# Sixteen conditioning slabs moved beside the latent attention, and the whole first feed-forward in seven products

## The chip, the cores and the metric

One core of one Trainium2 chip runs the kernel as a single program. The metric is the device time of one execution in microseconds (us); lower is better. Nothing is shared with other cores: all inputs come from HBM and the output goes back there.

## The reference, cut to what matters

The reference is two transformer-like blocks on one sequence of T = 512 tokens of width 1024, all in float32. What this change touches is the first block:

```
mod = silu(c) @ ada_w[layer] + ada_b[layer]          # per layer: 1024 -> 6 * 1024, "conditioning"
shift_m, scale_m, gate_m, shift_f, scale_f, gate_f = split(mod, 6)
h = rmsnorm(x, g) * (1 + scale_m) + shift_m
y = gated_delta_mixer(h) if layer == 0 else latent_attention(h)      # GDN / MLA
x = x + gate_m * y
h = rmsnorm(x, g2) * (1 + scale_f) + shift_f
x = x + gate_f * (silu(h @ w_gate) * (h @ w_up)) @ w_down            # D_FF = 2816
```

The second block (retention, sliding-window attention, a third feed-forward) follows and is not changed. The conditioning is a product of one row vector with a 1024 x 6144 matrix per layer: 24 slabs of 256 columns per layer, 48 in all, 1 MB each.

## The kernel before, in words

Everything is kept with channels on the 128 partitions and the 512 tokens along the free dimension. Weights come as slabs of 128 x 2048 float32 (1 MB), two in flight: `raw[0]`, `raw[1]`. Each slab is split into a rounded high half (`hi`, on ScalarE, `split_hi` L358) and the rest (`lo`, on VectorE, `split_lo` L364: raw minus hi, both in SBUF), and a product is three matmul passes, lo*H, hi*L, hi*H (`product`, L301 to L303). Semaphores order the engines: `lo_ready` counts split slabs, `slab_done` finished products, `bank_free` emptied accumulators. SyncE issues all DMAs in one written order: `load_slab` (L533) waits until the slab two before has been split, `load_ada` (L539) until PE has summed the conditioning slab two before it. A wait in that list holds back everything behind it.

A conditioning slab goes this way (`ada_chunks`, L369): DMA into `adar[0]` or `adar[1]`; GpSimd multiplies the 128 x 2048 tile by silu(c) (L373), then adds it up in three halvings, 1024, 512 and 256 wide (L375); PE sums the 128 partitions with two products against a column of ones (`ada_pe`, L523 to L531), each two passes, into columns of accumulator `D[3]`; VectorE adds the bias later (`mod_dve`) and makes the gains (`gain_cols`). Eight slabs of 48 are done at the start by another way, 40 by this one, numbered 2 to 41. Twenty run in the delta mixer, 2 to 21 (`ada_pool`, five per pair of heads, each pair's gated by VectorE), two are multiplied during its output product, and twenty, those two among them, are summed by PE one behind each of the first twenty slabs of the first feed-forward (numbers 22 to 41).

Each feed-forward has 34 slabs: 14 gate/up slabs, 8 down slabs, 8 gate/up slabs, 4 down slabs. The second and the third do the first two gate/up slabs as plain products and the other 12 and 8 by a Strassen-like scheme (`seven_pe`, L1709): seven quarter products of the slab halves and sums of halves, each 4 x 3 matmuls of 256 columns, plus extra splits, copies and sums on ScalarE and VectorE (`quick_pe`, `quick_act`, `quick_dve`). It needs the sums of the activations in `tH` and `tL`. In the first feed-forward (`ffn_pe` L2052, `ffn_act`, `ffn_dve`) only the last 8 gate/up slabs go that way; its first 14 are plain products, because `tH` lies in the same memory as `adar`, which is still in use by the conditioning.

Around it: `final_pe` (L594) is the output product of a mixer or the last down slabs of a feed-forward, with the squares of x for the next norm beside it. `close_act` and `close_dve` (L779) make the normed activation chunk by chunk and half by half: `nq` = x * gain * rstd (L789), `hH` on ScalarE, `hL` = `nq` + shift - `hH` (L796); PE's first product of the next stage (`product_halves`, L333 to L335) takes the chunks as they come. Before the attention, `mla_in_dve` computes the rope angles (L2136 to L2147), splits a slab, normalizes the latent (`craw`, `cL`, L2217, L2221) and turns the keys and queries (L2495 to L2497, L2531 to L2533).

The latent attention (`mla_pe` L2244) has 4 pairs of heads with 8 units each (2 heads x 4 blocks of queries). PE runs for each unit scores, then fills of the next pair's projections (`fill`), then the transpose of the probabilities of two units before (`turn`), then the values of three before. VectorE makes the maxima (from PSUM) and scales the probabilities (`pr` L2526); ScalarE makes the exponentials. Its last units alternate `turn`, `fill(1)` and `values`, where the fills are pieces of the output product's first slab.

## Time and profile before

| what | us |
| --- | --- |
| median of 3 runs (lowest, highest) | 2343.72 (2341.77, 2344.22) |
| the profiled execution, its own time | 2343.12 |
| its span, first to last instruction | 2341.3 |
| PE busy in the span | 2261.8 (97%) |
| DVE, ACT, POOL busy | 1397.7, 1034.7, 366.9 |

PE is TensorE's matmuls, PEld its weight loads, DVE VectorE, ACT ScalarE, POOL GpSimd and SP SyncE. POOL works in the first third of the span only. Stages, in us from the span's start: delta mixer to 425, its output product to 473, first feed-forward 473 to 850 (its plain gate/up slabs to 642, down to 723, sevens to 805, last down slabs behind), closing norm and latent input to 912, attention to 1046, its output product to 1081, second feed-forward 1081 to 1442. The mean granted clock of the core is 0.993.

### The profile page before, as it was taken

The numbers are of one execution on the slowest core, as the hardware profiler recorded it, in microseconds if no ns is written. First come the engines' busy times: TensorE is split into PE (matmuls) and PEld (weight loads), VectorE is DVE, ScalarE is ACT, GpSimd is POOL, SyncE is SP. The second block draws the span as 40 slices with busy tenths as digits, with TensorE's granted clock in tenths as the row PEclk, the third lists the DMA queues.
The fourth block names the chain that finished last, engine by engine and source line by source line (L and its number), as shares of the span: only waits on it lengthen the run. The fifth ranks groups of instructions, "written<-read, shape, count | busy, mean of one in ns | idle before, by whom it ended". The sixth has DMA issues, their size and how long they took to land.

```text
span 2341.3 us, 34757 instructions
## 1 busy us (share of the span) xinstructions
PE 2261.8 (97%) x14301; PEld 1916.9 (82%) x14301; DVE 1397.7 (60%) x1792; ACT 1034.7 (44%) x1545; POOL 366.9 (16%) x164
## 2 busy tenths in 40 slices
PE   6999999999999999999999999999999999999998
PEld 4777888888889986668998998888777788998897
DVE  4856755543347764546883676645467435984484
ACT  4546553443214544435552445334355324553352
POOL 0346447347790000000000000000000000000000
PEclk9999999999999999999999999999999999999999
DMA  7433232324452324311323232222211222233232
GB/s 293 149 113 136 100 135 91 118 117 180 180 210 90 114 73 162 126 64 63 104 105 116 90 127 97 90 72 72 90 55 55 85 96 73 91 109 126 90 109 90
DMA packets 40762, 260.56 MB, mean 111 GB/s; under 512 B 4432, under 2 KB 6832, under 8 KB 10416
## 3 DMA queue, kind: packets, MB, share of 16 engines
q1 hardware_dynamic: 40624, 258.59, 30.4%
q8 instruction: 103, 1.69, 0.3%
q14 instruction: 35, 0.29, 0.0%
HBM read 256.42 MB, written 2.15 MB: 110 GB/s over the span
## 4 chain that ended last, share of the span: by engine, by line
PE 79%; DVE 8%; ACT 5%; issue 2%; POOL 2%; DMA 0%; DVEq 0%; ACTq 0%
PE D L301 10%; PE D L302 10%; PE D L303 10%; PE D L1692 7%; PE D L1694 7%; PE D L1693 7%; PE D L1457 2%; PE D L2941 2%; PE D L1459 2%; PE D L1458 2%; DVE lo L366 1%; PE D L2943 1%; PE D L2942 1%; PE D L1476 1%; ACT hi L362 1%
## 5 line engine op out<-in xcount | busy, mean ns | idle before, releaser
L366 DVE TENSOR_TENSOR lo<-raw,hi 128x2048 fp32r<-128x2048 f32 (+3 forms) x131 | 290.0, 2214 | 198.8 <-ACT hi L362 198.6
L362 ACT ACTIVATE hi<-raw 128x2048 fp32r<-128x2048 f32 (+3 forms) x131 | 230.1, 1757 | 327.7 <-PE D L303 239.7
L301 PE MATMUL D<-hH,lo 128*128 128x512 f32 x560 | 227.9, 407 | 6.1 <-DVE lo L366 6.1
L303 PE MATMUL D<-hH,hi 128*128 128x512 f32 x560 | 221.3, 395 | 0.0
L302 PE MATMUL D<-hL,hi 128*128 128x512 f32 x560 | 221.3, 395 | 0.0
L1692 PE MATMUL D<-tH,lo 128*128 128x256 f32 x768 | 217.0, 283 | 0.5 <-issue 0.5
L1694 PE MATMUL D<-tH,hi 128*128 128x256 f32 x768 | 216.8, 282 | 0.0
L1693 PE MATMUL D<-tL,hi 128*128 128x256 f32 x768 | 216.5, 282 | 0.0
L375 POOL TENSOR_TENSOR adar<-adar 128x1024 f32<-128x1024 f32 (+2 forms) x120 | 212.4, 1770 | 9.4
L373 POOL TENSOR_TENSOR adar<-adar,small 128x2048 f32<-128x2048 f32 x40 | 154.9, 3874 | 324.9 <-DVE zi L1343 186.7
L1692 PE MATMUL D<-hH,lo 128*128 128x256 f32 x576 | 163.1, 283 | 2.3 <-ACT D L1775 2.3
L1694 PE MATMUL D<-hH,hi 128*128 128x256 f32 x576 | 162.6, 282 | 0.0
L1693 PE MATMUL D<-hL,hi 128*128 128x256 f32 x576 | 162.3, 282 | 0.0
L301 PE MATMUL D<-aH,lo 128*128 128x512 f32 x390 | 154.6, 396 | 0.0
L302 PE MATMUL D<-aL,hi 128*128 128x512 f32 x390 | 154.1, 395 | 0.0
L303 PE MATMUL D<-aH,hi 128*128 128x512 f32 x390 | 154.0, 395 | 0.0
L1692 PEld LDWEIGHTS D<-tH,lo 128*128 128x128 f32 x768 | 144.9, 189 | 1.1 <-issue 0.8
L1693 PEld LDWEIGHTS D<-tL,hi 128*128 128x128 f32 x768 | 145.0, 189 | 0.2
L1694 PEld LDWEIGHTS D<-tH,hi 128*128 128x128 f32 x768 | 144.8, 189 | 0.0
L301 PEld LDWEIGHTS D<-hH,lo 128*128 128x128 f32 x560 | 105.9, 189 | 33.5 <-DVE lo L366 7.9
L302 PEld LDWEIGHTS D<-hL,hi 128*128 128x128 f32 x560 | 105.8, 189 | 25.5 <-issue 2.4
L303 PEld LDWEIGHTS D<-hH,hi 128*128 128x128 f32 x560 | 105.6, 189 | 24.6
(547 smaller groups left out, 5438.8 us busy)
## 6 DMA issues: line engine op xcount, KB each, us to landing
raw<-in_slabs SPq DMA_DIRECT2D x185, 1024.0 KB, 4.8
adar<-in_ada SPq DMA_DIRECT2D x42, 1024.0 KB, 4.8
fw<-in_ada SPq DMA_DIRECT2D x6, 1024.0 KB, 23.3
x<-in_xin SPq DMA_DIRECT2D x2, 1024.0 KB, 8.9
dt<-bcast SPq DMA_DIRECT2D x8, 256.0 KB, 3.2
dtb<-bcast SPq DMA_DIRECT2D x8, 256.0 KB, 3.4
qd<-bcast SPq DMA_DIRECT2D x8, 256.0 KB, 3.6
out<-x SPq DMA_DIRECT2D x8, 256.0 KB, 2.2
```

What stands on the lines that cost most here:

```text
L301: T_.matmul(o, lo[s.slot][:, w], H[:, k, :], start=(k == 0), stop=False)
L302: T_.matmul(o, hi[s.slot][:, w], L[:, k, :], start=False, stop=False)
L303: last = T_.matmul(o, hi[s.slot][:, w], H[:, k, :], start=False, stop=(k == kc - 1))
L362: S_.activation(hi[s.slot][:, 0:n], raw[s.slot][:, 0:n], ACT.Copy).then_inc(hi_ready, 1)
L366: V_.tensor_tensor(lo[s.slot][:, 0:n], raw[s.slot][:, 0:n], hi[s.slot][:, 0:n], ALU.subtract).then_inc(lo_ready, 1)
L373: chain.link(nc.gpsimd.tensor_tensor(r3, r3, cact.unsqueeze(2).to_broadcast([P, KC, 2 * P]), ALU.mult))
L375: last = nc.gpsimd.tensor_tensor(r3[:, 0:n], r3[:, 0:n], r3[:, n:2 * n], ALU.add)
L1457: T_.matmul(o, lo[s % 2][:, c], hH[:, k, :], start=(k == 0), stop=False)
L1458: T_.matmul(o, hi[s % 2][:, c], hL[:, k, :], start=False, stop=False)
L1692: T_.matmul(to, w(lo, k), H(k), start=(fresh and k == 0), stop=False, skip_group_check=True)
L1693: T_.matmul(to, w(hi, k), L(k), start=False, stop=False, skip_group_check=True)
L1694: last = T_.matmul(to, w(hi, k), H(k), start=False, stop=(k == 3), skip_group_check=True)
```

## The change

Only slabs 22 to 25 of the conditioning are now summed by PE in the output product of the delta mixer. All that is left, 26 to 41 (parts of the second layer that its attention output and its feed-forward need), is loaded, multiplied and added up from the last down slabs of the first feed-forward on, through the closing norm, the latent input and the attention. The halvings end in a tile of their own, `adas`, which moves the attention's tiles up by 16 KB per partition, so that a load waits for GpSimd (`ada_sum`) and no more for PE. PE sums the sixteen in two groups of eight between the last units of the attention, and the four fill pieces move behind. The first feed-forward becomes `quick_*` with f = 0: 12 more slabs by seven products. The bias and the gains of the late parts are made behind the attention.

```diff
+ADA_MLA = 8 + 4 * ADA_P + 4 - ADA_SKEW
...
         mla = ExitStack()
+        adas = sb("adas", [P, 16, 2 * P], scope=mla)
...
-        def ada_chunks(pool, chain, a):
+        def ada_chunks(pool, chain, a, to=None):
...
+            for n in (4, 2):
+                chain.link(nc.gpsimd.tensor_tensor(r3[:, 0:n], r3[:, 0:n], r3[:, n:2 * n], ALU.add))
+            nc.gpsimd.tensor_tensor(r3[:, 0:1] if to is None else to, r3[:, 0:1], r3[:, 1:2],
+                                    ALU.add).then_inc(ada_sum, 1)
...
-            def body(i):
-                for j in range(2):
-                    ada_chunks(pool, chain, Slab(ADA0 + n + j, i, 2))
-            loop(pool, (2 * ADA_L - 8 - n) // 2, body, chain, 6)
+            for a in range(ADA0 + GH // 2 * ADA_P, ADA_MLA):
+                ada_chunks(pool, chain, Slab(a))
+            for k in range(16):
+                ada_chunks(pool, chain, Slab(ADA_MLA + k), adas[:, k:k + 1])
...
+        def ada_late_pe(pe, k):
+
+            pe.wait_ge(ada_sum, ADA_MLA + k + 1 - ADA0)
+            for m in range(2):
+                c = 3 * P + 2 * k + m
+                last = T_.matmul(D[3][:, 0, c:c + 1], adas[:, k, m * P:(m + 1) * P], ones[:, 0:1], start=True, stop=True)
+            last.then_inc(ada_done, 1)
...
         def load_ada(sp, a):
-            if a.b >= 2:
+            if a.b >= ADA_MLA + 2:
+                sp.wait_ge(ada_sum, a.plus(-1 - ADA0))
+            elif a.b >= ADA_MLA:
+                sp.wait_ge(slab_done, Slab(G_MIN - N_OUT - 1).plus(1))
+            elif a.b >= 2:
                 sp.wait_ge(ada_done, a.plus(-1))
...
-        def final_pe(pe, base, kc, H, L, ready, f, begun=False):
+        def final_pe(pe, base, kc, H, L, ready, f, begun=False, also=lambda j: None):
             for j in range(N_OUT - 1):
                 s = Slab(base + j)
+                also(j)
...
             for h in range(2):
+                also(N_OUT - 1 + h)
...
-        Q7 = lambda f, part: 2 * (N7[1] + (f - 1) * sum(N7) + part * N7[0])
-        RUN = lambda f, part: 2 * f + part - 1 if f else 0
+        Q7 = lambda f, part: 2 * (f * sum(N7) + part * N7[0])
+        RUN = lambda f, part: 2 * f + part
...
             g = base + NORD
+            if f == 0:
+                act.wait_ge(ada_done, ADA_MLA)
             diff_hi(act, f, 0)
...
-        def ffn_pe(pe, base, f, hb, n, ada_base=None):
...
             def turn(g):
-                w("pn", g + 1)
                 if g >= 2:
                     w("pt", g - 1)
+                w("pn", g + 1)
...
             turn(UALL - 1)
-            fill(1)
+            w("pt", UALL - 1)
+            for k in range(8):
+                ada_late_pe(pe, k)
             values(UALL - 2)
-            fill(1)
+            for k in range(8, 16):
+                ada_late_pe(pe, k)
             values(UALL - 1)
+            fill(2)
             fill(2)
...
-            ada1 = ADA0 + GH // 2 * ADA_P
+            load_ada(sp, Slab(ADA_MLA - 4))
+            load_ada(sp, Slab(ADA_MLA - 3))
             load_slab(sp, Slab(G_GOUT + 2))
+            load_ada(sp, Slab(ADA_MLA - 2))
             load_slab(sp, Slab(G_GOUT + 3))
-            load_ada(sp, Slab(ada1))
-            load_ada(sp, Slab(ada1 + 1))
-            load_slab(sp, Slab(G_FFN0))
-            load_slab(sp, Slab(G_FFN0 + 1))
-            left = 2 * ADA_L - ADA_SKEW - ada1 - 2
-            both(G_FFN0 + 2, ada1 + 2, left // 2, 2, (1, 1))
-            g = G_FFN0 + 2 + left
-            alone(g, G_MLA - g)
+            load_ada(sp, Slab(ADA_MLA - 1))
+            alone(G_FFN0, N_FFN)
+            late = iter(range(ADA_MLA, ADA_MLA + 16))
+            load_ada(sp, Slab(next(late)))
+            load_ada(sp, Slab(next(late)))
+            for j in range(N_MIN):
+                load_slab(sp, Slab(G_MIN + j))
+            load_ada(sp, Slab(next(late)))
+            load_ada(sp, Slab(next(late)))
             for p in range(GH // 2):
                 for k, src in enumerate((1, 0, 2, 3)):
                     load_slab(sp, mla_slab(p, k), G_MLA + PAIR * p + src)
+                    if (p, k) not in ((0, 0), (0, 2), (1, 0), (1, 1)):
+                        load_ada(sp, Slab(next(late)))
...
-            final_pe(pe, G_GOUT, KC, hH, hL, h_batch(pe, 1), 0)
-            ffn_pe(pe, G_FFN0, 0, 2, 1, ADA0 + GH // 2 * ADA_P)
+            final_pe(pe, G_GOUT, KC, hH, hL, h_batch(pe, 1), 0,
+                     also=lambda j: ada_pe(pe, Slab(ADA_MLA - 4 + j - j // 2 + j // 4), 1) if j != 2 else None)
+            quick_pe(pe, G_FFN0, 0, 1)
...
             def second_layer():
-                mod_dve(dve, chain, 6 * KC, 12 * KC, 2 * ADA_L - ADA_SKEW)
+                mod_dve(dve, chain, 6 * KC, 8 * KC, ADA_MLA, D[3][:, 1, 6 * KC:8 * KC])
                 dve.wait_ge(mod_ready, 2)
                 gain_cols(chain, 2, "mix_g", 1, 1)
-                gain_cols(chain, 3, "ffn_g", 1, 4)
-            ffn_dve(dve, chain, G_FFN0, 0, gate_col(0, 5), second_layer)
+            quick_dve(dve, chain, G_FFN0, 0, gate_col(0, 5), second_layer)
...
             mla_dve(dve, chain, 4)
+            mod_dve(dve, chain, 8 * KC, 12 * KC, ADA_MLA + 16, D[3][:, 0, 3 * P:3 * P + 4 * KC])
+            dve.wait_ge(mod_ready, 3)
+            gain_cols(chain, 3, "ffn_g", 1, 4)
             final_dve(dve, G_MOUT, gate_col(1, 2), 2)
```

## Rows read from the trace of the kernel before

**Rows 1.** The page, busy time, share and instructions of each engine.
```profile
PE 2261.8 (97%) x14301; PEld 1916.9 (82%) x14301; DVE 1397.7 (60%) x1792; ACT 1034.7 (44%) x1545; POOL 366.9 (16%) x164
```

**Rows 2.** Windows: stretch, length, busy PE, PEld, DVE, ACT, POOL, clock, DMA, GB/s.
```profile
491.05:837.03 345.98, 345.52 (x1855) 296.96 (x1855) 169.10 (x155) 118.04 (x128) 164.69 (x72) 1.00 0.41 155
1099.41:1426.18 326.77, 324.84 (x2212) 300.00 (x2213) 224.37 (x270) 148.38 (x217) 0.00 (x0) 1.00 0.30 107
```

**Rows 3.** Timeline of PE: start, duration, line, tiles, [idle before <- releaser].
```profile
437.27 0.50 PE L301 MATMUL D<-hH,lo 128*128 128x512 f32 x1 [0.60 <-DVE lo L366]
459.69 0.28 PE L611 MATMUL D<-hH,lo 128*128 128x256 f32 x1
502.34 0.50 PE L529 MATMUL D<-cst,adar 128*128 128x1 f32 x4
513.93 0.50 PE L529 MATMUL D<-cst,adar 128*128 128x1 f32 x4
```

**Rows 4.** Timeline of PE, end of the attention.
```profile
1044.53 0.50 PE L2248 MATMUL D<-hH,lo 128*128 128x512 f32 x1 [1.41 <-DVE hL L2509]
```

**Rows 5.** Timeline of POOL, one conditioning slab beside the first feed-forward.
```profile
519.39 3.60 POOL L373 TENSOR_TENSOR adar<-adar,small 128x2048 f32<-128x2048 f32 x1 [2.08 <-DMA adar<-in_ada]
523.07 4.57 POOL L375 TENSOR_TENSOR adar<-adar 128x1024 f32<-128x1024 f32 x3
```

**Rows 6.** Timelines of POOL and DVE where both work, delta mixer.
```profile
110.09 0.69 DVE L1360 COPY egl<-qd 128x8 f32<-128x8 f32 x1
314.87 3.61 POOL L373 TENSOR_TENSOR adar<-adar,small 128x2048 f32<-128x2048 f32 x1
315.37 4.18 DVE L1261 SCALAR_TENSOR_TENSOR qs<-qs,fs 128x1024 f32<-128x1024 f32 x1
359.11 3.60 POOL L373 TENSOR_TENSOR adar<-adar,small 128x2048 f32<-128x2048 f32 x1
361.43 4.63 DVE L1315 TENSOR_TENSOR go<-go,qs 128x512 f32<-128x512 f32 x2
365.99 3.35 DVE L366 TENSOR_TENSOR lo<-raw,hi 128x2048 fp32r<-128x2048 f32 x1
```

**Rows 7.** Windows over the delta mixer's output, the close, one attention pair.
```profile
425.10:437.20 12.10, 11.57 (x49) 8.83 (x47) 8.83 (x14) 8.59 (x12) 0.00 (x0) 1.00 0.07 31
848.95:877.85 28.90, 26.14 (x159) 22.73 (x157) 26.56 (x52) 17.63 (x28) 0.00 (x0) 1.00 0.10 37
952.00:984.40 32.40, 31.27 (x158) 21.68 (x158) 18.22 (x51) 13.15 (x35) 0.00 (x0) 1.00 0.38 130
```

**Rows 8.** Timelines of PE, SP and POOL: what sets when a slab arrives.
```profile
419.67 0.50 PE L529 MATMUL D<-cst,adar 128*128 128x1 f32 x4
437.62 0.91 SPq L542 DMA_DIRECT2D adar<-in_ada  x2
444.36 3.60 POOL L373 TENSOR_TENSOR adar<-adar,small 128x2048 f32<-128x2048 f32 x1 [35.15 <-DMA adar<-in_ada]
841.84 0.34 SPq L536 DMA_DIRECT2D raw<-in_slabs  x1
877.88 0.33 SPq L536 DMA_DIRECT2D raw<-in_slabs  x1
895.32 0.33 SPq L536 DMA_DIRECT2D raw<-in_slabs  x1
```

**Rows 9.** Timeline of DVE with POOL idle.
```profile
425.11 1.29 DVE L1315 TENSOR_TENSOR go<-go,qs 128x512 f32<-128x512 f32 x2 [1.93 <-ACT go L1093]
863.65 2.28 DVE L366 TENSOR_TENSOR lo<-raw,hi 128x2048 fp32r<-128x2048 f32 x1
885.66 2.08 DVE L2217 SCALAR_TENSOR_TENSOR craw<-craw,vec,pr 128x512 f32<-128x512 f32 x3 [4.20 <-ACT pr L2180]
904.27 0.69 DVE L2497 TENSOR_TENSOR qr<-qr,craw 128x512 f32<-128x512 f32 x1
942.71 0.49 DVE L2526 TENSOR_SCALAR pr<-pr,small 128x512 f32<-128x512 f32 x1
```

More of the change, by code:

```diff
@@ L373, in ada_chunks @@
             chain.link(nc.gpsimd.tensor_tensor(r3, r3, cact.unsqueeze(2).to_broadcast([P, KC, 2 * P]), ALU.mult))
-            for n in (4, 2, 1):
-                last = nc.gpsimd.tensor_tensor(r3[:, 0:n], r3[:, 0:n], r3[:, n:2 * n], ALU.add)
-                if n > 1:
-                    chain.link(last)
-            last.then_inc(ada_sum, 1)
+            for n in (4, 2):
+                chain.link(nc.gpsimd.tensor_tensor(r3[:, 0:n], r3[:, 0:n], r3[:, n:2 * n], ALU.add))
+            nc.gpsimd.tensor_tensor(r3[:, 0:1] if to is None else to, r3[:, 0:1], r3[:, 1:2],
+                                    ALU.add).then_inc(ada_sum, 1)
         def ada_pool(pool, chain):
-            n = GH // 2 * ADA_P
-            for k in range(n):
+            for k in range(GH // 2 * ADA_P):
                 if k % ADA_P == 0:
@@ L840, in gain_cols, with mod_dve @@
                 in1=vec[:, V[src] + KC * layer:V[src] + KC * layer + KC], op0=ALU.add, op1=ALU.mult))
-        def mod_dve(dve, chain, lo_, hi_, ada_n):
+        def mod_dve(dve, chain, lo_, hi_, ada_n, cols):
             dve.wait_ge(ada_done, ada_n)
-            V_.tensor_tensor(mod[:, lo_:hi_], D[3][:, 1, lo_:hi_], vec[:, V["ada_b"] + lo_:V["ada_b"] + hi_],
+            V_.tensor_tensor(mod[:, lo_:hi_], cols, vec[:, V["ada_b"] + lo_:V["ada_b"] + hi_],
                              ALU.add).then_inc(mod_ready, 1)
@@ L2049, in quick_dve @@
             final_dve(dve, g + 2 * N7[1], gate, 2 * f + 1)
-        def ffn_pe(pe, base, f, hb, n, ada_base=None):
-            hidden = lambda off, also: lambda k: hidden_pe(pe, 11 * f + off, k, also)
-            linear_pe(pe, base, N_GUA, KC, 2, hH, hL,
-                      lambda s: product_halves(pe, s, hb, {3: lambda: ones_half(pe, n - 1, 1)}), ada_base)
-            for j in range(N_DNA):
-                s = Slab(base + N_GUA + j)
-                if j == 0:
-                    product_first(pe, s, FA, 1, aH, aL, hidden(0, {}))
-                else:
-                    product(pe, s, FA, 1, aH, aL)
-                if ada_base + N_GUA + j < 2 * ADA_L - ADA_SKEW:
-                    ada_pe(pe, Slab(ada_base + N_GUA + j), 1)
-            base += N_GUA + N_DNA
-            close = sevens_pe(pe, base, Q7(f, 1), N7[1], lambda k: pe.wait_ge(h_ready, h_base(hb) + 2 * KC + k))
-            final_pe(pe, base + N_GUB, FB, aH, aL, hidden(FA // 2, {1: close}), n)
@@ L2068, in ffn_act @@
-        def ffn_act(act, base, f, nf):
-            def body(i):
-                s = Slab(base, i, 2)
-                act.wait_ge(slab_done, s.plus(1))
-                S_.activation(sg[:], D[s.slot][:], ACT.Silu).then_inc(bank_free[s.slot], 1)
-                split_hi(act, s.next(2))
-                u = s.next()
-                act.wait_ge(bank_free[u.slot], u.prior(1))
-                S_.activation(aH[:, bass.ds(at(0, i, 2), 2), :], af[:], ACT.Copy).then_inc(aH_ready, 1)
-                split_hi(act, u.next(2))
-            loop(act, N_GUA // 2, body)
-            g = base + N_GUA
-            for j in range(N_DNA - 2):
-                split_hi(act, Slab(g + j + 2))
-            act.wait_ge(ada_done, 2 * ADA_L - ADA_SKEW)
-            for k in range(4):
-                diff_hi(act, f, k)
-            g += N_DNA
-            before_act(act, g, Q7(f, 1))
-            sevens_act(act, g, Q7(f, 1), N7[1], 0)
-            final_act(act, g + N_GUB, nf)
@@ L3229, in _ @@
                     row_in(sp, qd, 2, p + 1, "eg_in")
-            def both(g, a, n, per, ada_per):
-                def body(i):
-                    k = 0
-                    for j in range(per):
-                        load_slab(sp, Slab(g + j, i, per))
-                        for _ in range(ada_per[j]):
-                            load_ada(sp, Slab(a + k, i, sum(ada_per)))
-                            k += 1
-                loop(sp, n, body)
             def alone(g, n):
@@ L3340, in _ @@
             close_act(act, G_GOUT, 0, 1, col(mod, MD(0, 3)))
-            ffn_act(act, G_FFN0, 0, 1)
+            quick_act(act, G_FFN0, 0, 1)
             close_act(act, G_MIN - N_OUT, 1, 2, col(mod, MD(1, 0)))
@@ L3369, in _ @@
             gdn_dve(dve, chain)
-            mod_dve(dve, chain, 2 * KC, 6 * KC, ADA0 + 2 * KC)
+            mod_dve(dve, chain, 2 * KC, 6 * KC, ADA0 + 2 * KC, D[3][:, 1, 2 * KC:6 * KC])
             dve.wait_ge(mod_ready, 1)
```

32 lines of the change are left out of this document (removed).

## The prediction

> **What bounds the kernel now.** First the page's busy shares: PE is busy for 97% of the span [rows 1], so a change gains what it takes from PE's stream and loses what it makes PE wait. Then I lay windows over stages, to compare the first feed-forward with the second, which already has the form that the first is to get [rows 2]. Then PE's own timeline, for the price of one product slab and of one column sum [rows 3]. Last POOL and DVE side by side, because the change moves POOL's work from a place where DVE is half idle to places where it isn't: the reader should see that two engines that never wait on each other by a semaphore still lengthen each other's instructions [rows 6].
>
> **The first feed-forward.** From the start of its second slab to its last down slabs it takes 345.98 us; the same stretch of the second takes 326.77 [rows 2]. The difference, 19.2, is the gain. It can be split. A plain product takes (459.69 - 437.27)/2 = 11.21 us; with a column sum behind it the pitch is 513.93 - 502.34 = 11.59, so a sum costs 0.38 [rows 3]. Twenty sums leave this stage, nineteen in the stretch: 7.2. The remaining 12.0 is 12 slabs by seven products, 1.0 each. DVE and ACT get more work there (224 and 148 us of 327 in the second), which leaves both below PE [rows 2], and SP's loads become those of the second.
>
> **Column sums that come back.** Four sums go into the delta mixer's output product. One falls into the wait before its second slab (0.60, for `lo`) [rows 3]; three are paid: 1.1. Sixteen stand at the end of the attention, 6.1, in place of the fill pieces, which now stand behind the last values and cover the wait of 1.41 for `hL` that is there now [rows 4]; I count 1.3 of it and take 4.8. The two tiny DVE operations of `mod_dve` and `gain_cols` go with this: they lie beside the fills. The exchange of the two waits in `turn` changes no order of work. So far -19.2 + 1.1 + 4.8 = -13.3.
>
> **What a conditioning slab does to DVE.** One slab is four POOL instructions, 3.60 for the product and 4.57 for the three halvings, 8.1 us in all when nothing disturbs it [rows 5]. The halvings take 2.4, 1.3 and 0.8 of it. Where DVE wants to read two tiles from SBUF meanwhile, it stands still until POOL's instruction is over: `qs<-qs,fs` started at 315.37, half a microsecond into a POOL product of 3.61, and took 4.18. Two products `go<-go,qs` took 4.63 at 361.43, against 1.29 for the pair with POOL idle, and the split behind them 3.35 against 2.28 [rows 6, 9]. Three DVE instructions in a row were each held up by a different POOL instruction. They take turns, one instruction each. So in a gapless run of such DVE operations, POOL's whole 8.1 us per slab is added to DVE's chain, less only DVE's idle time. A copy of 8 columns with a single SBUF input took 0.69, as long as a full 512 columns elsewhere [rows 6, 9], so it was held too; operations with an input in PSUM are the ones that I take as free. The nearest other reading is that the delay falls on POOL; that bounds the cost at zero. I take DVE, by these rows.
>
> By the Trainium skill ("SBUF — State Buffer", section "Who interferes with whom") a VectorE instruction with two SBUF inputs and a GpSimd instruction that reads SBUF exclude each other for the whole instruction, whichever came first. By that rule the turns would be the same; the trace agrees, with the 4.18 at 315.37.
>
> **Where the moved slabs fall.** (a) Delta mixer's output. The load of slab 23 waits for PE's sum of slab 21 at 419.67; a transfer takes some 5 us, so POOL starts near 425. Slab 24 may load as soon as PE has summed 22, at 425, and follows at once. Before, POOL was idle until 444.36 [rows 8]. DVE from 425.10 until PE gets its split at 437.2 is busy for 8.83 of 12.10 with `go`, `hL` and the split, nearly all of two SBUF inputs, and PE has no gap to give [rows 7, 3]. Two slabs hold 16.2, DVE's idle time takes 3.3: +12.9. Bounds 0 and 16.2.
>
> (b) Close and latent input. The loads of 28 and 29 stand right behind the raw load at 841.84. In the same constellation (issued at 437.62 behind a raw load) POOL began at 444.36, 6.7 us later [rows 8]; here that is 848.95. From there to 877.85 DVE is busy for 26.56 of 28.90 with `nq`, `hL`, a split, the rope angles and the split that PE's third slab needs [rows 7]. 16.2 - 2.3 = +13.9. PE has 2.8 of idle time in the same stretch, which is DVE's waiting already. Bounds 0 and 16.2. Slabs 26 and 27 come before it, beside the last down slabs, where a product lasts 11.2 us [rows 3] and a split of 2.3 [rows 9] has room: nothing, at most the 16.2 of the others.
>
> (c) Latent norm. The load of 30 follows the raw load at 877.88, and POOL starts near 885, just as DVE makes `craw` (three operations at 885.66) and then `cL` [rows 8, 9]. 8.1 less some 2.6 of slack before PE wants `cL`: +5.5. The load of 31 follows that at 895.32 and reaches POOL near 902.5, into the turning of keys and queries (0.69 each), where PE waits for DVE anyway; three of the four POOL instructions catch an operation: +5.0 [rows 8, 9]. Bounds 0 and 16.2 together.
>
> (d) Attention, ten slabs. In a pair DVE is busy for 18.22 of 32.40 [rows 7]: 14.2 idle. Fourteen operations per pair read SBUF only: four splits, two of the query turning, eight of `pr` (at most 0.49) [rows 9]. For the `pr` scalings no row shows a collision; the one-input copy is the nearest [rows 6], and I count them in. A random arrival while POOL runs finds, over pieces of 3.6, 2.4, 1.3 and 0.8, a mean rest of 1.3, so 14 x 1.3 = 18.2 per pair, 4.0 more than DVE has. Three pairs: +12. Bounds: 0, where all of it fits into the idle time, and 80.5 - 3 x 14.2 = 38, where every turn is lost.
>
> The skill's same section says that `copy`, `cast` and `tensor_scalar` can enter a two-port mode that excludes GpSimd too. By it the count of 14 would stand; were it not so, six operations would remain, 7.8 per pair, less than DVE's idle time, and (d) would be near nothing, 2367 in all. No run here shows it yet.
>
> **The sum.** 12.9 + 13.9 + 10.5 + 12 = 49.3 of DVE delay that reaches PE; with -13.3 it is +36.0. The profiled execution's own time is 2343.1 (span 2341.3), 0.6 below the median of 2343.7; 2343.1 + 36.0 = 2379.
>
> **The rivals.** B, on the other side: POOL is what waits. The twenty slabs ran beside the first feed-forward at 164.69 us of POOL and PE was busy for 345.52 of 345.98 [rows 2]: nothing there was lost. If DVE's delays stay in its slack at the new places too, the result is 2343.1 - 13.3 = 2330. It decides at 13.3 us: it is faster if less than that of the 49.3 reaches PE. Against it: that stage left DVE more than half idle, the stretches of (a) and (b) leave it 27% and 8%.
>
> C: only the gapless stretches collide, and only with one slab each, since the other arrives later than I read from the issue times: 6.5 + 7 + 10.5 = 24, with (d) at nothing: 2354.
>
> D: SP's list becomes the bound. In the last two pairs four loads per pair wait for POOL. POOL needs 4 x 8.1 and waits for DVE's fourteen operations, some 0.5 each [rows 9]: 39.8 us for a pair of 32.4. Two pairs are 14.8 behind, and raw slabs stand behind those loads in the list. One raw slab ahead covers a part; I take +12 on the forecast: 2391. For it: the arithmetic. Against: a stretched attention gives POOL the time.
>
> **How the numbers follow.** Forecast 58%, B 13%, C 17%, D 12%. Within 0.2% (4.7 us) a measurement can't be told from no change; that needs 13.3 of delay give or take 4.7, between B and C: 4%. Faster: 13%. Slower: 83%. The forecast's own range, with half to one and a half of (d) and 3 us each way in (a) and (b), is 2367 to 2391. The range of 8 in 10 goes down to 2350, to hold C, and up to 2402, the forecast with (d) near its upper bound; B and rests are left out.
>
> **What would show it.** Right: POOL busy near 425 to 441 and in the close, `nq`, `hL` and angles of 2 to 4 us instead of 0.5, PE idle in the close and latent input by some 24 us more, the first feed-forward's stretch at 327, DVE's busy time (waits included) up by tens of us, column sums of `adas` for 6 us. Wrong: `nq` and `hL` at 0.5 beside a working POOL (then B); POOL's slabs 28 and 29 starting behind the close (then C); SP waiting for POOL while ScalarE waits for raw slabs (then D). `pr` scalings at 0.5 beside POOL would take away most of (d) alone.

## The result, and the profile after

The changed kernel takes 2404.84 us (median of 4 runs, 2404.17 to 2406.5), the kernel before 2342.74 beside it (4 runs, 2340.95 to 2344.22). The ratio is 1.0267, 95% interval 1.0255 to 1.028: slower, as forecast, but by 62 us where 36 were forecast, and 2.8 us above the top of the range.

The page of the kernel after, the lines that answer to [rows 1]:

```profile
span 2404.3 us, 35692 instructions
PE 2275.4 (95%) x14735; PEld 1946.5 (81%) x14735; DVE 1521.5 (63%) x1908; ACT 1063.1 (44%) x1630; POOL 353.1 (15%) x164
PEclk9999999899999988898999999999999999999999
```

The span is 63.0 longer than the 2341.3 before. PE's share fell from 97% to 95%, but look at its busy time as well: it rose by 13.6 us, although 12.0 us of products are gone from the feed-forward. PE waits more, and it runs slower. The second is seen in the granted clock by stage. This clock has two levels in the traces, 1.2 and 2.4 GHz; the profile gives its mean over a window as a share of the higher one. Windows of the kernel after (busy us of PE, PEld, DVE, ACT, POOL, each with its count; then the granted clock, DMA share, GB/s), in order: PE's first product slab of the delta mixer's output; the first feed-forward's stretch of [rows 2]; close; latent input; attention; its tail up to the output product:

```profile
437.12:452.11 14.99, 14.99 (x56) 12.25 (x57) 2.59 (x3) 1.02 (x2) 8.05 (x4) 0.79 0.37 140
506.46:833.05 326.59, 324.66 (x2213) 300.05 (x2213) 227.92 (x269) 145.92 (x213) 18.28 (x7) 1.00 0.32 113
845.74:874.65 28.91, 19.47 (x105) 17.19 (x103) 27.50 (x33) 11.18 (x21) 15.82 (x8) 0.70 0.03 14
874.65:934.12 59.47, 45.47 (x173) 33.65 (x174) 39.55 (x42) 21.02 (x31) 17.92 (x8) 0.89 0.39 144
934.12:1089.38 155.26, 131.57 (x584) 89.11 (x582) 105.33 (x195) 51.79 (x131) 85.06 (x40) 0.91 0.42 162
1089.38:1107.83 18.45, 18.45 (x94) 17.78 (x95) 0.96 (x3) 1.20 (x2) 0.00 (x0) 0.63 0.00 1
```

The same stretches of the kernel before, from close to tail:

```profile
849.76:865.99 16.23, 13.87 (x104) 12.99 (x102) 14.44 (x32) 11.07 (x21) 0.00 (x0) 1.00 0.00 2
865.99:912.39 46.40, 42.90 (x173) 31.88 (x174) 26.52 (x42) 21.15 (x31) 0.00 (x0) 0.96 0.39 139
912.39:1039.50 127.11, 120.73 (x583) 81.85 (x582) 70.26 (x195) 51.25 (x131) 0.00 (x0) 0.99 0.32 115
1039.50:1046.02 6.52, 5.11 (x31) 4.39 (x32) 0.69 (x1) 1.19 (x2) 0.00 (x0) 1.00 0.00 1
```

In close, latent input and attention PE has the same instructions (its counts agree); the tail has the column sums besides. The stage lengths give the ledger, after less before: close 12.7, latent input 13.1, attention 28.2, tail 11.9. PE's timeline gives the rest: up to the first half product of the feed-forward, +15.4 (472.70 to 488.08; the delta mixer itself ended 1.7 earlier, so its output product lost 17.1); from there to the close's first half product -19.4; after the tail +1.1. The sum is 63.0. In close and latent input together PE's busy time grew by 64.94 - 56.77 = 8.2, in the attention by 10.8, with unchanged products: I read that part as the lower clock, the rest (17.6 and 17.3) is waiting.

Where PE waits first. PE's timeline of the kernel after (start, us, engine, line; in brackets the idle time before and who ended it):

```profile
437.12 1.02 PE L528 MATMUL D<-cst,adar 128*128 128x1 f32 x4 [13.31 <-DVE mod L857]
437.99 0.77 PE L318 MATMUL D<-hH,lo 128*128 128x512 f32 x1
438.56 0.63 PE L319 MATMUL D<-hL,hi 128*128 128x512 f32 x1
```

The first column sum of the mixer's output waits 13.31 us for `mod`, not for a slab, and the 512-column products behind it take 0.63 us, until 443.26, instead of 0.39. Who holds DVE in the attention: DVE's timeline, then POOL's, of the kernel after:

```profile
944.77 1.63 DVE L368 TENSOR_TENSOR lo<-raw,hi 128x512 fp32r<-128x512 f32 x1 [1.15 <-ACT hi L364]
946.32 1.76 DVE L2442 TENSOR_TENSOR craw<-qr,mcos 128x512 f32<-128x512 f32 x1
948.01 0.68 DVE L2443 TENSOR_TENSOR craw<-D,msin 128x512 f32<-128x512 f32 x1
948.72 4.05 DVE L2444 TENSOR_TENSOR craw<-craw 128x512 f32<-128x512 f32 x1
```

```profile
947.62 1.05 POOL L378 TENSOR_TENSOR adas<-adar 128x256 f32<-128x256 f32 x1
948.63 3.60 POOL L375 TENSOR_TENSOR adar<-adar,small 128x2048 f32<-128x2048 f32 x1
952.31 2.68 POOL L377 TENSOR_TENSOR adar<-adar 128x1024 f32<-128x1024 f32 x1
```

The addition at 948.72 begins 0.09 us behind POOL's product and ends behind it, at 952.77; without POOL it takes 0.69. The one before it, with an input in PSUM, takes 0.68 beside a working POOL, as always. PE stood for 5.30 us for that addition. PE's waits in the whole attention of the kernel after, the costliest (who waited for whom: us in all, times, longest):

```profile
PE D L2191 <- DVE craw L2444: 7.6, 2, 5.3
PE D L2191 <- DVE lo L368: 4.5, 2, 3.6
PE D L2292 <- DVE pr L2473: 4.4, 3, 2.0
PE D L2191 <- DVE qr L2444: 3.2, 1, 3.2
```

Groups of DVE instructions in the attention, first before, then after (count, busy us, mean ns):

```profile
L2526 DVE TENSOR_SCALAR pr<-pr,small 128x512 f32<-128x512 f32 x8 | 3.9, 488 | 0.3
L2497 DVE TENSOR_TENSOR craw<-craw 128x512 f32<-128x512 f32 x2 | 1.4, 692 | 0.1
```

```profile
L2473 DVE TENSOR_SCALAR pr<-pr,small 128x512 f32<-128x512 f32 x8 | 10.9, 1360 | 0.3
L2444 DVE TENSOR_TENSOR craw<-craw 128x512 f32<-128x512 f32 x2 | 7.4, 3715 | 0.1
L2465 DVE TENSOR_REDUCE small<-D 128x1 f32<-128x512 f32 x8 | 5.5, 691 | 0.3
```

So the scalings, of a single SBUF tensor, are held too; the maximum over PSUM is not (691 ns before as well).

### The profile page after: what moved, and what is told of

Its sections match the earlier page's. It is cut to its first block, busy times and chain, and to the rows that moved or that the text cites. A ratio compares the mean times of both kernels' runs of the same rounds, so it can differ in the third digit from the quotient of the medians.

```text
span 2404.3 us, 35692 instructions
## 1 busy us (share of the span) xinstructions
PE 2275.4 (95%) x14735; PEld 1946.5 (81%) x14735; DVE 1521.5 (63%) x1908; ACT 1063.1 (44%) x1630; POOL 353.1 (15%) x164
## 4 chain that ended last, share of the span: by engine, by line
PE 76%; DVE 11%; ACT 5%; issue 3%; POOL 1%; DMA 0%; DVEq 0%; ACTq 0%
PE D L1705 8%; PE D L1707 8%; PE D L1706 8%; PE D L303 8%; PE D L305 8%; PE D L304 8%; DVE lo L368 2%; PE D L1470 2%; PE D L2888 2%; PE D L1472 2%; PE D L1471 2%; PE D L2890 1%; PE D L2889 1%; PE D L1489 1%; PE D L318 1%
## 5 line engine op out<-in xcount | busy, mean ns | idle before, releaser
L364 ACT ACTIVATE hi<-raw 128x2048 fp32r<-128x2048 f32 (+2 forms) x118 | 205.3, 1740 | 346.6 <-PE D L305 237.3
L368 DVE TENSOR_TENSOR lo<-raw,hi 128x2048 fp32r<-128x2048 f32 (+2 forms) x118 | 266.3, 2257 | 136.7 <-ACT hi L364 136.6
L1705 PE MATMUL D<-tH,lo 128*128 128x256 f32 x960 | 270.5, 282 | 0.8 <-issue 0.8
L1707 PE MATMUL D<-tH,hi 128*128 128x256 f32 x960 | 270.4, 282 | 0.0
L1706 PE MATMUL D<-tL,hi 128*128 128x256 f32 x960 | 270.3, 282 | 0.0
L1706 PE MATMUL D<-hL,hi 128*128 128x256 f32 x720 | 202.7, 282 | 0.0
L377 POOL TENSOR_TENSOR adar<-adar 128x1024 f32<-128x1024 f32 x80 | 164.6, 2058 | 6.3
L303 PE MATMUL D<-hH,lo 128*128 128x512 f32 x368 | 151.8, 413 | 6.0 <-DVE lo L368 6.0
L305 PE MATMUL D<-hH,hi 128*128 128x512 f32 x368 | 146.2, 397 | 0.0
L304 PE MATMUL D<-hL,hi 128*128 128x512 f32 x368 | 146.1, 397 | 0.0
```

Of the source, the lines that this page charges most:

```text
L303: T_.matmul(o, lo[s.slot][:, w], H[:, k, :], start=(k == 0), stop=False)
L304: T_.matmul(o, hi[s.slot][:, w], L[:, k, :], start=False, stop=False)
L305: last = T_.matmul(o, hi[s.slot][:, w], H[:, k, :], start=False, stop=(k == kc - 1))
L364: S_.activation(hi[s.slot][:, 0:n], raw[s.slot][:, 0:n], ACT.Copy).then_inc(hi_ready, 1)
L368: V_.tensor_tensor(lo[s.slot][:, 0:n], raw[s.slot][:, 0:n], hi[s.slot][:, 0:n], ALU.subtract).then_inc(lo_ready, 1)
L377: chain.link(nc.gpsimd.tensor_tensor(r3[:, 0:n], r3[:, 0:n], r3[:, n:2 * n], ALU.add))
```

## The experiments

Theory T: POOL's arithmetic, by holding DVE, costs nearly all of the net loss; the loads, SP's list and the column sums cost little. Rivals are the loads and the list, and the clock or the sums by themselves. Stages are taken from each run's own trace, which is one execution. The kernel before took 2342.39 (12 runs) beside experiments 1, 2, 4 and 5, 2341.93 (13) beside 3, 6, 7 and 12, 2340.76 (9) beside 8 to 11 and 2341.17 us (18) beside 13 to 15. What comes back is counted from 2404.84.

**1. POOL silent for all sixteen late slabs.** In the silent kernels POOL only clears the slab's columns of `adas`, in place of `ada_chunks` for the slabs named. The product with silu(c) and the halvings are left out, so these kernels don't compute the late conditioning and show times only:

```
+ pool.wait_ge(ada_in[a.slot], a.prior(1, 16))
+ nc.gpsimd.memset(adas[:, k:k + 1], 0.0).then_inc(ada_sum, 1)
```

> The kernel after, but for the sixteen late slabs GpSimd only waits for the load and clears its 256 columns of `adas`; the product with silu(c) and the halvings of these slabs are left out, the 1 MB loads, SP's order and PE's column sums stay. Theory (POOL's reads hold up DVE): between the anchors of the two traces the closing norm lost 12.7 us, the latent input 13.1, the attention 28.2, together 54.0; all of it comes back, 2404.8 - 54.0 = 2351, and PE's granted clock in the attention is back at 0.98. Rival 1 (the sixteen extra loads, or SP's waits in its list, delay the raw slabs): nothing or little comes back, 2395 to 2405. Rival 2 (half of it is the clock, which falls because of the column sums and stays low): 2375 or more.

Measured: 2350.22 (2347.81 to 2352.54, 9 runs), ratio 1.0036 (1.0026 to 1.0046). 54.6 us come back with every load and sum in place. Close, latent input and attention take 16.2, 44.8 and 127.31 us, no longer than before, so T holds there and the loads cost nothing. The 8 us that are left are a net: the mixer's output +16.5, the feed-forward -19.5, the tail +11.9. One thing this run can't tell: with POOL silent, SP's list hardly waits for it either. For that, SP's wait for POOL in the attention of the kernel after:

```profile
SPq L553 <- POOL adas L378: 2.2, 2, 1.9
```

It is 2.2 us in all, and ACT waited for no raw slab there. The tail is as long as in the kernel after, and it shows the sums alone; the first window has slabs 1 to 8 of the sixteen, the second 9 to 16:

```profile
1035.11:1041.20 6.09, 6.09 (x42) 6.09 (x43) 0.00 (x0) 0.60 (x1) 0.00 (x0) 0.76 0.01 3
1041.20:1048.04 6.84, 6.84 (x35) 6.84 (x33) 0.00 (x0) 0.00 (x0) 0.00 (x0) 0.50 0.00 0
```

PE never waits inside them, and still the granted clock of the second is 0.50, the lower of its levels (1.2 GHz), while PE does little but load 128x128 weights for one column each: 6.84 us for eight slabs' sums.

**2. Silent for the four slabs of close and latent input (28 to 31).**

> The kernel after, with GpSimd's arithmetic left out for slabs 28 to 31 only (those that fall into the closing norm and the latent input). Theory (each slab hurts where it runs): 12.7 + 13.1 = 25.8 us come back and the attention keeps its 28.2: 2379. Rival (a delay in the close is only a shift: DVE would have waited later anyway, or the attention absorbs it): less than 15 come back, 2390 or more.

Measured: 2369.56 (2362.03 to 2374.58, 4 runs), ratio 1.0104 (1.0082 to 1.0125). 35.3 come back, 9.5 more than I expected and against the rival. Close and latent input fall to 61.1 us (62.6 before), and the attention, with all ten of its slabs, loses 21.1 instead of 28.2.

**3. Silent for the ten slabs of the attention (32 to 41).**

> GpSimd's arithmetic is left out for the ten late slabs that run beside the attention (32 to 41), and their column sums see zeros; loads, order and sums stay, and slabs 26 to 31 keep their arithmetic. The two earlier runs without arithmetic gave back 54.6 us (all sixteen slabs) and 35.2 us (the four of close and latent input). By the ledger of PE's timeline the attention lost 28.2 us by its own collisions: 2404.8 - 28.2 = 2376.6, and the two parts then overlap by some 9 us (28.2 + 35.2 - 54.6), since the slabs beside the close make the attention start late into the same traffic. Rival: the parts add, the attention's share is only what the earlier run leaves, 54.6 - 35.2 = 19.4, and the time is 2385.4. A granted clock of 1.00 through the attention is expected by the first.

Measured: 2379.27 (2378.07 to 2380.8, 4 runs), ratio 1.0162 (1.0146 to 1.0179): 25.5 come back, between the two. In its trace the attention takes 125.73 us at a clock of 1.00, 29.5 less than after, but the tail takes 21.68 at 0.53 where it was 18.45 at 0.63: the clock takes 3.2 of it back. The two parts overlap by 25.5 + 35.3 - 54.6 = 6 us.

**4. The sums of the mixer's output one place later.** The sum before the first slab goes, the four stand before slabs 2, 3, 4 and the last half:

```
- also=lambda j: ada_pe(pe, Slab(ADA_MLA - 4 + j - j // 2 + j // 4), 1) if j != 2 else None)
+ also=lambda j: ada_pe(pe, Slab(ADA_MLA - 5 + j), 1) if j else None)
```

> The kernel after, with the four column sums in the delta mixer's output product each one place later (before its second slab, its third, and the two halves of its last), so that PE's first product there no longer stands behind the wait for `mod_ready`. Theory (PE's wait of 13.3 us for the first `mod_dve` was the loss, as the trace of after shows): 10 to 13 come back, 2392 to 2395. Rival (my forecast: slabs 23 and 24 on POOL hold up DVE, and PE would wait for `hL` and the split instead): at most 3 come back, 2402 or more.

Measured: 2393.21 (2392.44 to 2394.75, 4 runs), ratio 1.0217 (1.02 to 1.0234): 11.6 come back, as expected. By its trace that size is partly luck: the stage itself gave 8.9, the attention, which was not touched, another 5.9, and the tail took 3.2 back. Its PE timeline shows what is POOL's own doing there, while slab 23 was on POOL:

```profile
431.94 0.80 PE L318 MATMUL D<-hH,lo 128*128 128x512 f32 x1 [5.32 <-DVE hL L1333]
```

5.32 us of waiting inside the first slab, and the stage ends 6.5 later than before instead of 15.4.

**5. The late sums spread.** Four behind the last but one `values`, twelve in three groups between the slabs of the attention's output product, the fills back in their places, `mod_dve` in two parts:

```
+ if 1 <= j <= 3:
+     pe.wait_ge(mod_ready, 3)
+     for k in range(4 * j, 4 * j + 4):
+         ada_late_pe(pe, k)
```

> The kernel after, with four late column sums between the last units of the attention and the other twelve between the slabs of its output product, four before each of the last three pieces; the fill pieces stand where they were before the change. Theory (thirty-two products of one column in a row let the granted clock fall to half, and they take twice as long; between slabs of 512 columns the clock stays): of the 11.9 us that the tail lost, 5 to 7 come back, 2398 to 2400, with the clock at 1.00 there. Rival (the sums cost 0.38 each wherever they stand, and the rest was the missing cover for the last waits): 1 or 2 come back, 2403 to 2404, the clock as low as in after.

Measured: 2398.55 (2394.64 to 2402.41, 4 runs), ratio 1.0243 (1.0224 to 1.0263): 6.3 come back. Windows of its sums:

```profile
1105.14:1106.98 1.84, 1.84 (x18) 1.84 (x17) 1.41 (x2) 1.59 (x1) 0.00 (x0) 1.00 0.00 0
```

Four slabs' sums take 1.84 at a clock of 1.00, 0.46 a slab, against 6.84 / 8 = 0.86 at 0.50. From the last `turn` to the final slab of the output product it loses 7.0, where the kernel after loses 11.9.

**6. Both repairs.**

> Both repairs at once: the four sums of the delta mixer's output one slab later, and the late sums spread between product slabs with the fills back in their places. If the two are independent their gains add: 11.6 + 6.3, 2404.8 - 17.9 = 2386.9. Rival: the earlier start of the first feed-forward lets the later stages meet GpSimd differently and part of it is lost again: above 2392.

Measured: 2392.46 (2391.91 to 2395.14, 4 runs), ratio 1.0218 (1.0201 to 1.0235): 12.4 instead of 17.9; it lies at the rival's bound, but the interval of experiment 5 alone is 4.6 us each way, so that they don't add is likely and not certain. In the trace its attention takes 155.06, as long as after, where the repairs one by one had 149.3 and 147.5. From trace to trace the attention's loss lies between 20 and 28 us, with no change made to it. I put that down to how POOL's instructions happen to fall on DVE's; no run isolates it.

**7. POOL's work in pieces.** Same work, no instruction over 512 columns, in the sixteen late slabs:

```
+ for k in range(0, KC, 2):
+     chain.link(nc.gpsimd.tensor_tensor(r3[:, k:k + 2], r3[:, k:k + 2],
+                cact[:, k:k + 2].unsqueeze(2).to_broadcast([P, 2, 2 * P]), ALU.mult))
+ for k in (0, 2):
+     chain.link(nc.gpsimd.tensor_tensor(r3[:, k:k + 2], r3[:, k:k + 2], r3[:, k + 4:k + 6], ALU.add))
```

> Each late slab's product is cut into four instructions of 512 columns and its first halving into two of 512, so no GpSimd instruction lasts much over 1.3 us; the sum of its work is the same. Where VectorE runs without gaps the turns take GpSimd's whole time all the same, so close and latent input stay as they are (25.8 us). Where VectorE's operations arrive at random, the mean rest of a GpSimd instruction falls from 1.3 to 0.5 us, and the attention's loss of 28.2 falls in proportion to about 11: 2388 (2380 to 2395). Rival: what counts is GpSimd's busy time in all, not the length of one instruction: 2400 or more.

Measured: 2375.09 (2371.66 to 2378.06, 4 runs), ratio 1.0142 (1.0125 to 1.0159): 29.7 come back, more than expected and below the range I gave. The length of one hold counts, not POOL's total, which rose:

```profile
926.32:1059.88 133.56, 122.95 (x584) 83.46 (x582) 84.39 (x195) 51.92 (x131) 97.93 (x80) 0.97 0.50 188
```

The attention loses 6.5 instead of 28.2, beside 97.93 us of POOL instead of 85.06. Close and latent input lose 17.0 instead of 25.8; I had expected no gain where DVE has no gaps. The cut has a price of its own: SP's list now waits for POOL, 67.3 us in the attention where it was 2.2, and ScalarE waited once, 2.4 us, for a raw slab. DVE in the close, first of the kernel after, then in pieces:

```profile
845.16 3.88 DVE L802 SCALAR_TENSOR_TENSOR nq<-x,gsc,nrs 128x256 f32<-128x256 f32 x1
848.96 2.56 DVE L809 SCALAR_TENSOR_TENSOR hL<-nq,mod,hH 128x256 fp32r<-128x256 f32 x1
```

```profile
850.02 1.26 DVE L812 SCALAR_TENSOR_TENSOR nq<-x,gsc,nrs 128x256 f32<-128x256 f32 x1
854.02 1.51 DVE L819 SCALAR_TENSOR_TENSOR hL<-nq,mod,hH 128x256 fp32r<-128x256 f32 x1
```

**8. Both repairs and pieces.**

> Both repairs and the late slabs' GpSimd work in pieces of at most 512 columns. The pieces gave back 29.7 us by themselves, the two repairs together 12.3. Independent of each other: 2404.8 - 29.7 - 12.3 = 2363. Rival: with the attention near its undisturbed length the repairs count in full again (11.6 + 6.3): 2357. Above 2368 would say that the pieces and the repairs gave back partly the same time.

Measured: 2362.86 (2358.08 to 2370.1, 4 runs), ratio 1.0084 (1.0068 to 1.0101). The first expectation. It is the best version with the first feed-forward by seven products that computes everything, and still 22 us slower than before. Its clock was low in the tail all the same, with only four sums there:

```profile
1050.50:1063.50 13.00, 11.59 (x46) 10.37 (x47) 0.76 (x2) 1.20 (x2) 0.00 (x0) 0.55 0.01 1
```

The same order ran at 1.00 in the profiled executions of experiments 5, 6, 10 and 11, and at 0.52 in that of 12. In 8 and 12 the clock was low before the first of the four sums, so they did not start its fall; in 12 the first fill behind the wait for `pr` already took 0.63.

**9. The kernel before in pieces.** The same cut for every slab of the kernel before.

> The kernel before with every slab's product in four and its first halving in two GpSimd instructions, nothing else. Twenty of its slabs run beside the first feed-forward, where TensorE waited for nothing, and the others beside the delta mixer, where some VectorE operations are held. Expected 2340, within 2335 to 2342: the cut helps only where VectorE is TensorE's bound. Rival: more and dependent GpSimd instructions delay the column sums in the delta mixer, and it gets slower, 2345 or more.

Measured: 2353.84 (2352.08 to 2356.75, 5 runs), ratio 1.0056 (1.0042 to 1.007): slower, the rival. Lines of POOL, of the kernel before and in pieces, the product in each:

```profile
L373 POOL TENSOR_TENSOR adar<-adar,small 128x2048 f32<-128x2048 f32 x40 | 154.9, 3874 | 324.9 <-DVE zi L1343 186.7 <-DMA adar<-in_ada 138.2
```

```profile
L374 POOL TENSOR_TENSOR adar<-adar,small 128x512 f32<-128x512 f32 x160 | 192.9, 1206 | 279.8 <-DVE zi L1345 181.7 <-DMA adar<-in_ada 88.5
```

Four pieces cost 4.8 us where one product cost 3.9. POOL too is held at its turns (the shortest of its 512-column products took 1.03, the longest 3.16), and beside the delta mixer and the first feed-forward it becomes the engine that PE waits for, at a column sum, 8.6 us in all where it was 0.5:

```profile
689.33 0.64 PE L531 MATMUL D<-cst,adar 128*128 128x1 f32 x4 [1.70 <-POOL adar L380]
```

**10. Repairs, and all slabs in pieces; 11. the same in instructions of 256 columns.**

> As mended_pieces, with the delta mixer's and its output's slabs cut as well. Slabs 23 and 24 hold VectorE's hL of the mixer's output: by the repaired kernel's timeline 6.5 us are still lost there, half of which should come back, and what before_pieces gains in the mixer: 2363 - 3 - 2 = 2358. Rival: TensorE's column sums wait longer for the cut slabs in the mixer: 2363 or more.

> As all_pieces, but in instructions of 256 columns: eight products, four, two and one additions. If the length of one hold is what costs, the mean rest falls once more (0.5 to some 0.3 us) and a third of what is still lost in close, latent input and attention (some 25 us) comes back: 2350. Rival: with 15 instructions instead of 8 the fixed part of each and the larger number of turns eat it up: the same as all_pieces or slower.

Measured: 2363.29 (2359.53 to 2369.32, 4 runs), ratio 1.0102 (1.0086 to 1.0118), the same as experiment 8 and just on the rival's side; and 2395.92 (2394.21 to 2397.3, 4 runs), ratio 1.0234 (1.0219 to 1.025), 33 slower, the rival. With 256 columns PE waits for POOL's sums for 18.1 us in all (5.1 in experiment 10), as here in the mixer:

```profile
319.82 1.01 PE L531 MATMUL D<-cst,adar 128*128 128x1 f32 x4 [3.05 <-POOL adar L382]
```

and enters the feed-forward's half product at 504.40 instead of 482.82; its attention, 147.7, is 13.8 longer as well. That is rival D of the forecast, come true here: SP waited 84.2 us for POOL in it, ScalarE waited four times for a raw slab, 15.7 us, and PE's longest wait, 7.7, is for the `lo` of such a slab. Of the three sizes tried, the middle one is the best: instructions short enough for DVE, and few enough for POOL and for SP's list behind it.

**12. Repairs, and POOL silent for the sixteen.**

> Both repairs and no arithmetic of GpSimd for the sixteen late slabs (their column sums see zeros). It shows what the change would bring with its by-products gone: 2350.2 - 10 (wait for the modulation, by PE's timeline) - 4.9 (the sums at a higher granted clock) = 2335, some 7 us below the kernel before; the rest against 2342.4 - 19.4 = 2323 is the sixteen and four column sums and the delay of slabs 23 and 24, which keep their arithmetic. Rival: something else of the change costs PE time, then it stays above 2342.

Measured: 2338.74 (2335.57 to 2341.01, 10 runs), ratio 0.9985 (0.9976 to 0.9995). Even with POOL's late work for nothing, and both by-products repaired, the change gains some 3 us, a little less than the 7 that I expected. By PE's timeline it is -19.4 in the feed-forward, 5.5 still lost in the mixer's output, and 12.8 in tail and output product, with a clock of 0.52 in the tail. So hiding POOL's work better would not have made this change worth much.

**13 to 15. The tail alone.** Open was whether the sums, their order or the disturbed attention made the tail slow. The kernel before, with only this at the end of its attention (the rest of the sixteen behind `values(UALL - 2)` in the same way); in experiment 14 without the products, in 15 with `ones` of 128 columns in place of one:

```
  turn(UALL - 1)
- fill(1)
+ w("pt", UALL - 1)
+ for k in range(8):
+     for m in range(2):
+         c = 3 * P + 2 * k + m
+         T_.matmul(D[3][:, 0, c:c + 1], ident, ones[:, 0:1], start=True, stop=True)
  values(UALL - 2)
- fill(1)
...
  values(UALL - 1)
+ fill(2)
  fill(2)
```

> The kernel before, with the attention's end of the kernel after and nothing else of the change: 32 one-column products with 128x128 weights stand in two runs of sixteen where the late column sums stand (of other data, written where nobody reads), the fills behind them. Nothing of GpSimd differs. If these products lower the granted clock, as the tail of the kernel after showed it (18.45 us instead of 6.52), it takes 2340.8 + 12 = 2353, with a clock of 0.5 in the tail. Rival: the clock fell because of the waits of an attention disturbed by GpSimd, and the sums cost 0.4 a slab: 2347, at a clock of 1.00.

> As before_sums without the products: only the order of the tail, the wait for `pt` and the fills behind the last values. By the units' timeline the fills no longer cover the wait behind the last turn, some 1 us, and cover the 1.41 for hL: 2341 (2339 to 2344), clock 1.00. Rival: the order alone, with its wait before the last values, already lowers the clock: 2346 or more.

> As before_sums, but every one of the 32 products has 128 columns instead of one. A product of 128 columns takes about twice 0.11 us in the delta mixer's timeline, 32 of them 7.0 us. If it is the single column that lets the clock fall, it stays at 1.00 here and the kernel takes 2341 + 7 = 2348, less than with one column: more work in less time. Rival: the place decides, whatever stands there: the clock falls as in before_sums, 14 us for the products, 2355 or more.

Measured: with one column 2356.34 (2353.59 to 2356.61, 4 runs), ratio 1.0067 (1.005 to 1.0083); order alone 2341.04 (2336.79 to 2342.32, 10 runs), ratio 0.9999 (0.999 to 1.0009); with 128 columns 2347.56 (2345.85 to 2349.15, 9 runs), ratio 1.0027 (1.0017 to 1.0037). Windows from the last `turn` to the product, in this order, one fence for each kernel:

```profile
1035.34:1057.03 21.69, 21.69 (x95) 20.80 (x95) 0.69 (x1) 1.19 (x2) 0.00 (x0) 0.53 0.00 1
```

```profile
1037.32:1042.74 5.42, 5.38 (x30) 4.32 (x31) 0.69 (x1) 1.19 (x2) 0.00 (x0) 1.00 0.01 2
```

```profile
1035.32:1049.22 13.90, 13.89 (x94) 13.02 (x95) 0.69 (x1) 1.20 (x2) 0.00 (x0) 0.88 0.01 2
```

By their times, all three first expectations. The one-column products cost 15 us, 32 of them, with nothing of the rest of the change; their order costs nothing. The same number with 128 columns costs 6.4: more work in less time. The clock is lower there too, a mean of 0.88, where I had expected 1.00. What starts its fall is another question. PE's timeline of experiment 13, then of experiment 15, then the whole tail of experiment 9, which has no such products:

```profile
1035.34 0.99 PE L2349 MATMUL D<-cst,pr 128*128 128x128 f32 x4 [1.94 <-DVE pr L2534]
1036.12 6.83 PE L2390 MATMUL D<-cst 128*128 128x1 f32 x32
```

```profile
1035.82 5.36 PE L2390 MATMUL D<-cst 128*128 128x128 f32 x32
1041.69 3.74 PE L2395 MATMUL D<-cst 128*128 128x128 f32 x32
```

```profile
1047.49:1055.60 8.11, 6.70 (x30) 5.72 (x31) 0.69 (x1) 1.19 (x2) 0.00 (x0) 0.79 0.00 1
```

In 13 the clock was already low at the last `turn`, whose four small products took 0.99 instead of 0.66, before the first one-column product. In 9 it fell at the same place, and came back within some 4 us. Behind the one-column products it does not come back while they last: the second run of sixteen took 6.83 at 0.50 in every trace that has two such runs (after, experiments 1 to 4, 7 and 13), while with 128 columns the second run took 3.74 at 1.00. So the one-column products hold the low clock; whether they also start the fall (in the kernel after it came partway through the first run, 4.81) the runs don't settle.

## Why the prediction was right and wrong

**First feed-forward, -19.2: right.** The stretch takes 326.59 us; its model, the second feed-forward, took 326.77 [rows 2].

**(a) Mixer's output, 12.9 + 1.1: near in size by luck, wrong cause.** The ledger has 15.4. The step that failed is that a column sum costs PE 0.38 and nothing more. `ada_pe(pe, ..., 1)` waits for `mod_ready`, which DVE gives only behind all of `hL`; standing before the first slab, it took away the overlap of that slab with `hL`. Experiment 4 gave 8.9 of the stage back. Of DVE's delay itself only 5.3 us reached PE there: slab 23 did collide (POOL 423.39 to 432.5), slab 24 came at 442.96, after the stretch, not at once behind 23 as I had read from the issue times.

**(b) and (c) Close and latent input, 13.9 + 10.5: right in sum (25.8), with a part that was not in it.** POOL came at 845.15, 0.6 us before the close (forecast: 848.95, 0.8 before the old close at 849.76), `nq` took 3.88 and `hL` 2.56, and experiment 2 shows all of it gone with four slabs silent. But 8.2 of the 25.8 are PE at a lower clock, and waits are 17.6 where I had 24.4. The turns, one instruction each, hold; that they cost POOL's whole time in a gapless run does not, by experiment 7: the same turns in shorter pieces cost a third less.

**(d) Attention, 12: wrong, 28.2.** The step that failed is the subtraction, "14 x 1.3 = 18.2 per pair, 4.0 more than DVE has". The forecast had 54.6 us of delay in three pairs and let idle time pay for 42.6 of it. Measured, DVE was busy for 105.33 us instead of 70.26, a delay of only 35.1, less than the 56.9 that it had idle before; by the subtraction PE would have lost nothing, and it waited 17.3 us longer. Idle time of DVE in one unit does not pay for a delay in another: DVE's work comes in bursts (split, turning of a query or key, then scalings), and PE waits at the end of a burst. The two additions into `craw` took 4.05 and 3.38 us instead of 0.69, held for more than the mean rest of 1.3: one arrived 0.09 us behind the start of a long product, the other 1.2 us into one, and PE waited 5.30 and 2.32 us for them. The inclusion of the scalings was right (488 to 1360 ns). By the Trainium skill ("SBUF — State Buffer", section "Who interferes with whom") a `tensor_scalar` can enter a mode that takes both of VectorE's ports and then excludes GpSimd. The trace agrees with that, by the 1360 ns. The second part is the clock: PE busy for 10.8 us longer at 0.91. Experiments 3 and 7 return 29.5 and 21.7 of the stage. With the same instructions in the attention, the traces of experiments 4 to 6 lose 22, 20 and 28 us there, so no single number could have been exact.

**Tail, 4.8: wrong, 11.9.** The term was 16 x 0.38 from a sum that stands between product slabs at full clock [rows 3]. That price was the failed step: sixteen in two runs stood at a clock of 0.50 for most of their time, with POOL silent (experiment 1) and in the kernel before (13). At a clock of 1.00 the sixteen would cost 16 x 0.46 = 7.4, about what experiment 5 lost (7.0). Cover of 1.3 by the fills was there (14: the tail alone is 1.1 shorter).

**Rivals.** B (POOL waits) did not hold in the changed kernel, but it is half true of the same mechanism: in experiments 9 and 11 POOL's instructions stretch until PE waits for them. C did not hold: slabs 28 and 29 both collided. D was not seen: SP waited 2.2 us for POOL in the attention, DVE's idle time ahead of its small splits, which follows a late raw slab, fell from 6.0 to 3.2 us, and PE's longest waits there end at DVE's `craw`, `qr` and `lo`. With POOL's work cut finer it appears, in experiment 11. (D's sum, with the numbers it shows, is 39.4 us a pair and not 39.8.)

**The range.** By terms, the 27.0 us that the trace has above the forecast are 16.2 in the attention, 7.1 in the tail and 3.7 in the rest. What the forecast had nowhere is PE's clock. In the attention it fell behind the waits of 5.30, 3.57 and 3.24 us, where the kernel before had none above 1.94. By busy times it cost 2.2 us in the mixer's output (the first slab takes 13.93 instead of 11.77), 8.2, 10.8, and some 5 in the tail, 26 in all. That this equals the gap between 2379 and 2405 is chance: in close and latent input the clock's 8.2 stood in place of 6.8 us of waits that I had too many. No stage has the clock's share isolated by an experiment. In the tail it is the difference between sums at 0.86 and at 0.46 a slab; in the other stages it is read from busy times, and it left with the waits (experiment 3: attention at 1.00).

## What to carry to other kernels

Work put on GpSimd "beside" another stage is free only where VectorE's SBUF-only operations have room there, burst by burst; cut its instructions there, to the length of VectorE's own and no further, and leave them whole where VectorE is not what TensorE waits for (experiment 9 lost 13 us by the cut). Before a small TensorE instruction is moved, list every semaphore that its helper waits for, and put it where none of them is young. When a change makes TensorE wait or gives it one-column products in a row, add the clock: here 9% on TensorE's busy time in the attention and 14% in close and latent input together, and about double on a run of one-column products; measure a small product's cost where it will stand, not between large ones.

## What the runs showed of the hardware

In the kernel after, a 512-column `tensor_scalar` in SBUF took up to 3.91 us beside GpSimd (0.49 alone); the nine groups of attention operations with an input in PSUM took what they take alone, within 2%. GpSimd is held likewise: its final halving of 256 columns, 0.73 alone, took 1.05 in the attention and 1.18 on the mean in experiment 9. With thirty-two one-column products with 128x128 weights (64 in the records) the clock was at 0.50 without a wait among them, and in experiment 13 it stayed low for 5 us behind them. The same tail ran at either level: four of six profiled executions with the sums spread had 1.00, two 0.52 and 0.55. After a wait of 13.31 us the next 15 us ran at a mean clock of 0.79, the first 6 of them at the lower level.
